# A hybrid decoder trunk on one core: all row loads ahead of the first panels, and a first pair in the order of its operands

## The chip, the cores and the metric

The kernel runs on one core of a Trainium2 chip. The metric is the device time in microseconds, as the median of several executions. The kernel before takes 1883.57 us (three runs, 1883.14 to 1888.67).

## The reference

Two layers over 256 tokens of width 1024, batch 1. Each sub-layer normalises, modulates by a condition c, mixes, gates and adds. What this case touches is the very beginning, the first sub-layer of layer 0:

```python
c_act = jax.nn.silu(c)
mod = c_act @ ada_w[0] + ada_b[0]                 # 6 * 1024 numbers
sh1, sc1, g1, sh2, sc2, g2 = jnp.split(mod, 6, axis=-1)
h = rms_norm(x, tok_norm[0]) * (1 + sc1) + sh1
b_gate, c_gate, v = jnp.split(h @ w_in, 3, axis=-1)   # w_in: 1024 x 3072
u = c_gate * v                                    # then a causal convolution of width 3
x = x + g1 * ((b_gate * conv(u)) @ w_out)
```

A channel mixer follows (product-key retrieval over 16384 experts), then the second layer with latent attention and a second channel mixer. They make up most of the time and are not changed.

## The kernel before

All is laid out with channels on the 128 partitions and 256 tokens along the free axis, so the activation is eight blocks of 128x256. A weight matrix comes as *panels* of 128x1024 f32 (512 KB): one panel holds the eight 128x128 blocks for 128 output channels. Products are made in float32r with a split: each panel is cast to a high part `w_hi` (ScalarE, `split_hi`, L1007) and the rest `w_lo` = panel minus high part (GpSimd, `split_lo`, L1353); the activation is split the same way into `act_hi` and `act_lo`. A panel is then 24 matmuls of 128x256: high by high, high weights by low activation, low weights by high activation. There are four raw slots, four slots for high and two for low panels. SyncE issues a panel's load when the low part of the panel four before it is made (`load`, L378).

The modulation is computed on VectorE as 1024-long dot products with silu(c): each *ada row* (128x1024 f32, 512 KB) gives 128 numbers (`ada_row`, L1429). Six slots hold the rows, so `load_ada(n, ...)` (L388) waits until row n - 6 has been used. Rows 0 to 7 give the scales sc1, rows 8 to 15 the shifts sh1; further rows come three by three among the panels.

The opening, engine by engine:

- SyncE (L448 to L468) issues c, row 0, x, the constants, rows 1 to 11, panels 0 and 1 of `conv_in`, rows 12 to 15, panels 2 and 3. Then a loop of three rows and three panels at a time.
- ScalarE (L1207 to L1237) makes silu(c), the squares of x and the root, copies the spread 1/rms, casts panels 0 and 1, multiplies the eight blocks by the gains (L1225), adds the shifts while it casts to `act_hi` (`normalise`, L1034), and casts panel 2. The shifts come in two halves of four blocks (semaphore `scaled`).
- VectorE (L1974 to L1993) takes the rows, makes the gains after row 7, the first four shifts after row 11, the last four after row 15, and then the low activation (`normalised_lo`, L1462). In the panel stage it consumes the products and takes further rows between.
- GpSimd (L1370 to L1381) multiplies x by 1/rms in two halves and then makes the low panels in order.
- TensorE (L989 to L996) bridges its waits by products of zeros (`busy`, L615). The first two panels are multiplied together by `first_pair` (L537): high and low weights by the first four blocks of `act_hi` for both panels, five products of zeros, the same for the other four blocks, and last the high weights by `act_lo`. Panels 2 to 23 follow by `full_panel` (L583), one after the other in two banks, then the output projection. `PAIRS_IN_ORDER` (L106) tells GpSimd in which stages the first two panels are multiplied as such a pair, whose low slots are free before the product is done (`pair_lo_used`).

The lines that set the opening's order on TensorE and in SyncE's queue are these:

```python
for j in range(KB // 2):
    load_ada(KB + j, j, (KB + j) % ADA)
for j in range(2):
    load_panel("conv_in", j)
for j in range(KB // 2, KB):
    load_ada(KB + j, j, (KB + j) % ADA)
...
busy(PAN[0], 50)
first_pair(norm_hi, norm_ready, 0, lambda p: wait_panel("conv_in", p), fill=5)
for j in range(2, 24):
    full_panel("conv_in", j)
```

Of the kernel before, what the change touches and what calls it, by code (L numbers as in the profile page):

```python
# [30 lines left out]
P = 128  # L31
D = 1024
KB = D // P
T = 256
# [10 lines left out]
RAW = 4  # L45
HI, LO = 4, 2
HI_LEAD = HI - 1
ADA = 6
# [56 lines left out]
MLA_ORDER = (3, 4, 5, 6, 0, 1, 2)  # L105
PAIRS_IN_ORDER = ("conv_in", "conv_out", "sel0", "mla_in", "mla_out", "sel1")  # L106
QB_ORDER = (4, 5, 0, 1, 2, 3)
# [8 lines left out]
def program(nc, xT_in, c_in, pos_in, vec_in, con_in, ada_in, pan_in, key_in, iota_in, u_in, v_in, out):  # L116
    ctx = ExitStack()
    grid = [nc.dram_tensor(f"gates_by_expert{l}", (KEYS * KEYS * P, 1), F32, kind="Internal").ap() for l in range(2)]
    with ctx:
# [257 lines left out]
        def _(sp):  # L377
# [7 lines left out]
            def load_panel(stage, j, unroll=0, it=0, width=D):  # L385
                load(pan_in, it * unroll + (DENSE[stage] + j), stage, j, unroll, it, width)
# [66 lines left out]
            for j in range(1, KB):  # L453
                load_ada(j, KB + j, j % ADA)
            for j in range(KB // 2):
                load_ada(KB + j, j, (KB + j) % ADA)
            for j in range(2):
                load_panel("conv_in", j)
            for j in range(KB // 2, KB):
                load_ada(KB + j, j, (KB + j) % ADA)  # L460
            for j in range(2, RAW):
                load_panel("conv_in", j)
# [33 lines left out]
        def _(pe):  # L496
# [39 lines left out]

            def first_pair(hi, lo, count, wait, acts=norm_act, fill=0):  # L537

                slots = []
                for half in range(2):  # L540
                    if half:
                        busy(STAT, fill)
                    pair_hi(hi, count, slots, acts, half * KB // 2, (half + 1) * KB // 2, wait if half == 0 else None)
                pair_lo(lo, count, slots, acts)

            def conv_pair():
# [445 lines left out]
            spread_rstd(1)  # L992
            busy(PAN[0], 50)
            first_pair(norm_hi, norm_ready, 0, lambda p: wait_panel("conv_in", p), fill=5)
            for j in range(2, 24):
# [10 lines left out]
        def _(act):  # L1006
# [26 lines left out]

            def normalise(n, l, s0):  # L1034

                for k in range(KB):
                    act.wait_ge(scaled, KB * (n - 1) + k + 1)
# [180 lines left out]
            nc.scalar.copy(rstd[:, T:2 * T], STAT[:, T:2 * T]).then_inc(rstd0_copied, 1)  # L1218
            for j in range(2):
                split_hi("conv_in", j)  # L1220
            act.wait_ge(gains0, 1)
# [4 lines left out]
            act.wait_ge(by_gain, KB)  # L1226
            normalise(1, 0, 0)
            split_hi("conv_in", 2)
            for it in range(2):
# [907 lines left out]
```

## Time and profile before

| | |
|---|---|
| median of three runs | 1883.57 us (1883.14, 1883.57, 1888.67) |
| the profiled execution | 1886.6 us, its span 1884.8 us |
| TensorE busy | 1866.2 us, 99% of the span |
| VectorE, ScalarE, GpSimd busy | 1492.7, 1001.2 and 783.3 us |
| transfers | 388.82 MB, mean 206 GB/s |
| TensorE's first panel product | at 32.42 us |
| end of the first stage's 24 panels | at 104.65 us |

The span is the time between the first and the last instruction that the profile holds; the execution's own time is a little longer. A panel of 24 matmuls takes 2.88 us at the full clock. PE, ACT, DVE, POOL and SP stand for TensorE, ScalarE, VectorE, GpSimd and SyncE.

### The profile page before, as it was taken

The page shows a single profiled execution, that of the slowest core. Times are in us where ns is not written, and L with a number is a line of the kernel's source. Part 1 is how long each engine was busy: PE and PEld are TensorE (multiplying, and loading weights), DVE is VectorE, ACT ScalarE, POOL GpSimd, SP SyncE. Part 2 cuts the span into 40 slices and gives each one's busy share as a digit, 9 for nine tenths or more (in the row PEclk, how much of TensorE's full clock was granted, in tenths as well). Part 3 has the DMA queues.
Part 4 walks back from the last instruction along what each step waited for, and adds up shares of the span by engine and source line. Part 5 has one row for each costly group of instructions (what it writes and reads, how often), then busy time and mean ns, then how long its engine had stood idle before and what let it go on. Part 6 is the DMA issues. An engine that isn't in the chain of part 4 may idle for free.

```text
span 1884.8 us, 37910 instructions
## 1 busy us (share of the span) xinstructions
PE 1866.2 (99%) x12642; PEld 1655.2 (88%) x12642; DVE 1492.7 (79%) x2893; ACT 1001.2 (53%) x1598; POOL 783.3 (42%) x378
## 2 busy tenths in 40 slices
PE   8999999999999999999999999999999999999999
PEld 7999998888888888887789999988888888888887
DVE  6758999999778977997765489988887678668866
ACT  4354555555555555554454645555555555555553
POOL 3877548788860000000062575487888820000000
PEclk8999999999999999999998999999999999999999
DMA  9986657898897777876632565577777776667664
GB/s 352 364 271 202 187 136 185 229 225 230 229 244 245 257 233 236 264 233 225 223 114 83 170 200 168 136 159 182 184 179 189 190 215 194 187 193 215 190 191 140
DMA packets 174340, 388.82 MB, mean 206 GB/s; under 512 B 48801, under 2 KB 84001, under 8 KB 173857
## 3 DMA queue, kind: packets, MB, share of 16 engines
q1 hardware_dynamic: 120960, 379.01, 64.0%
q0 software_dynamic: 36864, 0.15, 4.7%
q10 hardware_dynamic: 16416, 8.39, 1.6%
q8 instruction: 56, 0.92, 0.2%
q14 instruction: 44, 0.35, 0.1%
HBM read 377.92 MB, written 9.57 MB: 206 GB/s over the span
## 4 chain that ended last, share of the span: by engine, by line
PE 92%; DVE 4%; DMA 2%; ACT 1%; issue 1%; POOL 1%; DVEq 0%; SPq 0%; ACTq 0%; POOLq 0%
PE bank L673 36%; PE bank L658 18%; PE bank L663 9%; PE bank L637 6%; PE bank L642 6%; PE bank L638 6%; PE bank L692 2%; PE bank L704 1%; DMA raw<-in_v_panels 1%; PE bank L720 1%; PE bank L522 1%; PE bank L502 1%; PE bank L953 1%; PE bank L504 1%; PE bank L503 1%
## 5 line engine op out<-in xcount | busy, mean ns | idle before, releaser
L1012 ACT CAST w_hi<-raw 128x1024 fp32r<-128x1024 f32 (+1 forms) x603 | 630.5, 1046 | 327.9 <-PE bank L673 104.0
L1414 DVE TENSOR_TENSOR w_lo<-raw,w_hi 128x1024 fp32r<-128x1024 f32 x488 | 596.9, 1223 | 192.4 <-PE bank L673 88.5
L1389 POOL DMA_INDIRECT gates_by_expert<-g_t,place x256 | 504.9, 1972 | 190.0 <-DVE place L1713 76.4
L1361 POOL TENSOR_TENSOR w_lo<-raw,w_hi 128x1024 fp32r<-128x1024 f32 (+2 forms) x115 | 273.3, 2380 | 528.3 <-PE bank L673 381.4
L658 PE MATMUL bank<-act_two,w_hi 128*128 128x512 f32 x1536 | 379.3, 389 | 0.0
L658 PEld LDWEIGHTS bank<-act_two,w_hi 128*128 128x128 f32 x1536 | 288.3, 188 | 59.8
L673 PE MATMUL bank<-w_hi,wt_hi 128*128 128x512 f32 x1024 | 325.5, 398 | 1.9 <-DVE wt_lo L1676 1.2
L673 PE MATMUL bank<-w_lo,wt_hi 128*128 128x512 f32 x1024 | 317.9, 391 | 0.0
L673 PE MATMUL bank<-w_hi,wt_lo 128*128 128x512 f32 x1024 | 317.0, 390 | 0.0
L637 PE MATMUL bank<-act_two,w_hi 128*128 128x256 f32 x984 | 246.1, 288 | 0.0
L638 PE MATMUL bank<-act_two,w_hi 128*128 128x256 f32 x984 | 241.2, 283 | 0.0
L673 PEld LDWEIGHTS bank<-w_hi,wt_lo 128*128 128x128 f32 x1024 | 192.3, 188 | 41.9
L673 PEld LDWEIGHTS bank<-w_lo,wt_hi 128*128 128x128 f32 x1024 | 192.2, 188 | 41.8
L663 PEld LDWEIGHTS bank<-act_two,w_lo 128*128 128x128 f32 x1536 | 209.5, 190 | 15.0
L663 PE MATMUL bank<-act_two,w_lo 128*128 128x256 f32 x1536 | 213.9, 282 | 0.0
L673 PEld LDWEIGHTS bank<-w_hi,wt_hi 128*128 128x128 f32 x1024 | 178.1, 189 | 32.0 <-issue 4.2
L1065 ACT COPY ring_g<-bank 128x256 f32 (+1 forms) x192 | 71.7, 374 | 253.1 <-PE bank L663 245.1
L638 PEld LDWEIGHTS bank<-act_two,w_hi 128*128 128x128 f32 x984 | 188.5, 192 | 0.0
L637 PEld LDWEIGHTS bank<-act_two,w_hi 128*128 128x128 f32 x984 | 188.2, 191 | 0.0
L642 PE MATMUL bank<-act_two,w_lo 128*128 128x256 f32 x984 | 138.5, 283 | 0.0
L642 PEld LDWEIGHTS bank<-act_two,w_lo 128*128 128x128 f32 x984 | 127.2, 192 | 0.0
L1631 DVE TENSOR_TENSOR hot_b<-ib_t,iota 128x2048 bf16<-128x2048 bf16 x96 | 116.9, 1218 | 0.8 <-PE bank L704 0.8
(257 smaller groups left out, 1951.2 us busy)
## 6 DMA issues: line engine op xcount, KB each, us to landing
raw<-in_u_panels SPq DMA_DIRECT2D x256, 512.0 KB
raw<-in_v_panels SPq DMA_DIRECT2D x256, 512.0 KB
raw<-in_panels SPq DMA_DIRECT2D x81, 512.0 KB
ada<-in_ada_rows SPq DMA_DIRECT2D x56, 512.0 KB
arena<-in_ada_rows SPq DMA_DIRECT2D x40, 512.0 KB, 7.0
gates_by_expert<-zero ACTq DMA_DIRECT2D x2, 4096.0 KB, 22.2
arena<-gates_by_expert SPq DMA_DIRECT2D x32, 256.0 KB, 5.3
gates_by_expert<-g_t,place POOLq DMA_INDIRECT x256
```

What stands on the lines that cost most here:

```text
L637: pe.matmul(bank, w_hi[:, hi_slot, w], acts[0][k], start=(k == 0), stop=False)
L638: pe.matmul(bank, w_hi[:, hi_slot, w], acts[1][k], start=False, stop=False)
L642: mm = pe.matmul(bank, w_lo[:, lo_slot, w], acts[0][k], start=False, stop=(k == KB - 1))
L658: pe.matmul(bank[:, 0:2 * T], w_hi[:, hi_slot, w], act_two[:, :, a], start=(k == 0), stop=False, skip_group_check=True)
L663: mm = pe.matmul(bank[:, 0:T], w_lo[:, lo_slot, w], act_hi[:, a], start=False, stop=(k == KB - 1), skip_group_check=True)
L673: mm = pe.matmul(YB[2 * t + n][:], wt[:, par, a], (w_hi, w_lo)[v][:, slots[v], n * 512:(n + 1) * 512], start=False, stop=False, skip_group ...
L1012: nc.scalar.copy(w_hi[:, slot, 0:width], raw[:, slot, 0:width]).then_inc(hi_done, 1)
L1065: nc.scalar.copy(ring_g[:, bass.ds(slot * T, T)], bank[:, T:2 * T]).then_inc(lo_copied, 1)
L1361: pool.tensor_tensor(w_lo[:, lo_slot, 0:width], raw[:, slot, 0:width], w_hi[:, slot, 0:width].bitcast(F32), ALU.subtract).then_inc(lo_done, 1)
L1389: pool.indirect_dma_start(grid[l], bass.IndirectOffsetOnAxis(place[:, n:n + 1], 0), kept[:, n:n + 1], None, compute_op=ALU.add).then_inc(a ...
L1414: dve.tensor_tensor(w_lo[:, lo_slot, 0:width], raw[:, slot, 0:width], w_hi[:, slot, 0:width].bitcast(F32), ALU.subtract).then_inc(lo_done, 1)
L1631: dve.tensor_tensor(wide(hot_b[:, par, :]), each(ib_t, KEYS, token0), numbers(0, KEYS), ALU.is_equal)
```

## The change

SyncE issues all sixteen ada rows ahead of the first panel. ScalarE no longer casts panels 0 and 1 before it multiplies by the gains: it multiplies, normalises the first four blocks, casts panel 0, normalises the other four blocks and casts panels 1 and 2. TensorE multiplies the first two panels by a function of its own, `opening_pair`: panel 0's high weights by the high and then by the low activation, the same for panel 1, then the low weights of both. There are 56 products of zeros ahead of it instead of 50, and none within it. As this pair's low slots are now released by `pan_done`, `conv_in` leaves `PAIRS_IN_ORDER`; `first_pair` keeps its form for the other stages. The number of products, casts and loads is otherwise the same, and VectorE's and GpSimd's order too.

```diff
--- before.py
+++ after.py
@@ -103,7 +103,7 @@
 
 WIDTHS = {BASE["q_b"] + _j: 2 * Q_LORA for _j in range(6)} | {BASE["k_b"] + _j: 2 * KV_LORA for _j in range(4)}
 MLA_ORDER = (3, 4, 5, 6, 0, 1, 2)
-PAIRS_IN_ORDER = ("conv_in", "conv_out", "sel0", "mla_in", "mla_out", "sel1")
+PAIRS_IN_ORDER = ("conv_out", "sel0", "mla_in", "mla_out", "sel1")
 QB_ORDER = (4, 5, 0, 1, 2, 3)
 TWO_PI = 2.0 * np.pi
 sq_before = {1: 0, 3: TT}
@@ -452,13 +452,9 @@
             sp.dma_start(vec[:], vec_in).then_inc(s_const, 16)
             for j in range(1, KB):
                 load_ada(j, KB + j, j % ADA)
-            for j in range(KB // 2):
+            for j in range(KB):
                 load_ada(KB + j, j, (KB + j) % ADA)
-            for j in range(2):
-                load_panel("conv_in", j)
-            for j in range(KB // 2, KB):
-                load_ada(KB + j, j, (KB + j) % ADA)
-            for j in range(2, RAW):
+            for j in range(RAW):
                 load_panel("conv_in", j)
             with sp.Fori(0, 2) as it:
                 for b in range(4):
@@ -534,14 +530,35 @@
                         mm = pe.matmul(PAN[p][:, 0:T], w_hi[:, s[0], w], acts[1][k], start=False, stop=(k == KB - 1))
                     mm.then_inc(pan_done, 1)
 
-            def first_pair(hi, lo, count, wait, acts=norm_act, fill=0):
+            def first_pair(hi, lo, count, wait, acts=norm_act):
 
                 slots = []
                 for half in range(2):
-                    if half:
-                        busy(STAT, fill)
                     pair_hi(hi, count, slots, acts, half * KB // 2, (half + 1) * KB // 2, wait if half == 0 else None)
                 pair_lo(lo, count, slots, acts)
+
+            def opening_pair():
+
+                hi, lo, acts = norm_hi, norm_ready, norm_act
+                for p in range(2):
+                    slot, _, _, n = ring("conv_in", p)
+                    pe.wait_ge(evac["conv_in"], p + 1)
+                    pe.wait_ge(hi_done, n)
+                    for k in range(KB):
+                        if p == 0:
+                            pe.wait_ge(hi, k + 1)
+                        pe.matmul(PAN[p][:, 0:T], w_hi[:, slot, k * P:(k + 1) * P], acts[0][k], start=(k == 0), stop=False)
+                    for k in range(KB):
+                        if p == 0:
+                            pe.wait_ge(lo, k + 1)
+                        pe.matmul(PAN[p][:, 0:T], w_hi[:, slot, k * P:(k + 1) * P], acts[1][k], start=False, stop=False)
+                for p in range(2):
+                    _, lo_slot, _, n = ring("conv_in", p)
+                    pe.wait_ge(lo_done, n + RAW)
+                    for k in range(KB):
+                        mm = pe.matmul(PAN[p][:, 0:T], w_lo[:, lo_slot, k * P:(k + 1) * P], acts[0][k], start=False,
+                                       stop=(k == KB - 1))
+                    mm.then_inc(pan_done, 1)
 
             def conv_pair():
 
@@ -990,8 +1007,8 @@
             pe.wait_ge(s_const, 48)
             token_square_sums(1)
             spread_rstd(1)
-            busy(PAN[0], 50)
-            first_pair(norm_hi, norm_ready, 0, lambda p: wait_panel("conv_in", p), fill=5)
+            busy(PAN[0], 56)
+            opening_pair()
             for j in range(2, 24):
                 full_panel("conv_in", j)
             conv_pair()
@@ -1031,9 +1048,9 @@
                 nc.scalar.activation(rms[:, 0:TT], STAT[:, 0:TT], ACT.Sqrt, bias=eps[:], scale=1.0 / D
                                      ).then_inc(rms_ready, 1)
 
-            def normalise(n, l, s0):
-
-                for k in range(KB):
+            def normalise(n, l, s0, k0=0, k1=KB):
+
+                for k in range(k0, k1):
                     act.wait_ge(scaled, KB * (n - 1) + k + 1)
                     c = l * 48 + s0 * KB + k
                     nc.scalar.activation(act_hi[:, k * T:(k + 1) * T], act32[:, k * T:(k + 1) * T],
@@ -1216,16 +1233,17 @@
             rms_of(1)
             act.wait_ge(rstd_spread, 1)
             nc.scalar.copy(rstd[:, T:2 * T], STAT[:, T:2 * T]).then_inc(rstd0_copied, 1)
-            for j in range(2):
-                split_hi("conv_in", j)
             act.wait_ge(gains0, 1)
             for k in range(KB):
                 act.wait_ge(by_rstd, 1 + k * 2 // KB)
                 c = slice(k * T, (k + 1) * T)
                 nc.scalar.activation(act32[:, c], act32[:, c], ACT.Copy, scale=gain[:, k:k + 1]).then_inc(by_gain, 1)
             act.wait_ge(by_gain, KB)
-            normalise(1, 0, 0)
-            split_hi("conv_in", 2)
+            normalise(1, 0, 0, 0, KB // 2)
+            split_hi("conv_in", 0)
+            normalise(1, 0, 0, KB // 2, KB)
+            for j in range(1, HI_LEAD):
+                split_hi("conv_in", j)
             for it in range(2):
                 for b in range(4):
                     for j in range(3):
```

SyncE's queue at the opening, before (arena<-in_ada_rows is a row, raw<-in_panels a panel):

```order
L448 DMA crow<-in_c 128x1024
L391 DMA arena<-in_ada_rows 128x1024 [waits ada_rows_used]
L450 DMA xT<-in_xT 128x2048
L451 DMA con<-in_constants 128x256
L452 DMA vec<-in_vectors 128x164
L391 DMA arena<-in_ada_rows 128x1024 [waits ada_rows_used] x11
L382 DMA raw<-in_panels 128x1024 [waits panel_lo_ready] x2
L391 DMA arena<-in_ada_rows 128x1024 [waits ada_rows_used] x4
L382 DMA raw<-in_panels 128x1024 [waits panel_lo_ready] x2
```

and with the change:

```order
L448 DMA crow<-in_c 128x1024
L391 DMA arena<-in_ada_rows 128x1024 [waits ada_rows_used]
L450 DMA xT<-in_xT 128x2048
L451 DMA con<-in_constants 128x256
L452 DMA vec<-in_vectors 128x164
L391 DMA arena<-in_ada_rows 128x1024 [waits ada_rows_used] x15
L382 DMA raw<-in_panels 128x1024 [waits panel_lo_ready] x4
```

Panels 0 and 1 moved behind rows 12 to 15; nothing else in the queue moved.

ScalarE from the copy of 1/rms on, before (L1225 multiplies by the gains, L1039 adds the shifts and casts):

```order
L1218 COPY ring_g<-bank 128x256 [waits token_rstd_spread]
L1012 CAST w_hi<-raw 128x1024 [waits panel_multiplied,panel_landed0]
L1012 CAST w_hi<-raw 128x1024 [waits panel_multiplied,panel_landed1]
L1225 ACTIVATE ring_g<-ring_g,gain 128x256 [waits x_by_rstd_ready,first_gains_ready]
L1225 ACTIVATE ring_g<-ring_g,gain 128x256 [waits x_by_rstd_ready] x7
L1039 ACTIVATE act_two<-ring_g,mod 128x256 [waits x_scaled,x_by_gain_ready]
L1039 ACTIVATE act_two<-ring_g,mod 128x256 [waits x_scaled] x7
L1012 CAST w_hi<-raw 128x1024 [waits panel_multiplied,panel_landed2]
```

and with the change (the same lines are now L1235, L1029, L1240 and L1056):

```order
L1235 COPY ring_g<-bank 128x256 [waits token_rstd_spread]
L1240 ACTIVATE ring_g<-ring_g,gain 128x256 [waits x_by_rstd_ready,first_gains_ready]
L1240 ACTIVATE ring_g<-ring_g,gain 128x256 [waits x_by_rstd_ready] x7
L1056 ACTIVATE act_two<-ring_g,mod 128x256 [waits x_scaled,x_by_gain_ready]
L1056 ACTIVATE act_two<-ring_g,mod 128x256 [waits x_scaled] x3
L1029 CAST w_hi<-raw 128x1024 [waits panel_multiplied,panel_landed0]
L1056 ACTIVATE act_two<-ring_g,mod 128x256 [waits x_scaled] x4
L1029 CAST w_hi<-raw 128x1024 [waits panel_multiplied,panel_landed1]
L1029 CAST w_hi<-raw 128x1024 [waits panel_multiplied,panel_landed2]
```

Both casts moved behind the scaling, and the first of them between the two halves of the normalisation.

TensorE's first pair, before (L618 are the products of zeros, L522 and L523 high and low weights by the high activation, L534 high weights by the low activation):

```order
L618 MATMUL bank<-zero 128x512 x50
L522 MATMUL bank<-act_two,w_hi 128x256 [waits normalised_hi_ready,evacuated_conv_in,panel_lo_ready]
L523 MATMUL bank<-act_two,w_lo 128x256
...
L618 MATMUL bank<-zero 128x512 x5
...
L534 MATMUL bank<-act_two,w_hi 128x256 [waits normalised_split] x8
L534 MATMUL bank<-act_two,w_hi 128x256 x8
```

and with the change (L635 zeros, L550 high by high, L554 high weights by the low activation, L559 low weights):

```order
L635 MATMUL bank<-zero 128x512 x56
L550 MATMUL bank<-act_two,w_hi 128x256 [waits normalised_hi_ready,panel_hi_ready,evacuated_conv_in]
L550 MATMUL bank<-act_two,w_hi 128x256 [waits normalised_hi_ready] x7
L554 MATMUL bank<-act_two,w_hi 128x256 [waits normalised_split] x8
L550 MATMUL bank<-act_two,w_hi 128x256 [waits panel_hi_ready,evacuated_conv_in]
L550 MATMUL bank<-act_two,w_hi 128x256 x7
L554 MATMUL bank<-act_two,w_hi 128x256 x8
L559 MATMUL bank<-act_two,w_lo 128x256 [waits panel_lo_ready]
L559 MATMUL bank<-act_two,w_lo 128x256 x7
```

The pair's first product now waits for a high panel and no low one, and the 16 products with low weights moved from between the others to the end.

## Rows read from the trace of the kernel before

**Rows 1.** The page's part 4: the chain that ended last, by engine.

```profile
PE 92%; DVE 4%; DMA 2%; ACT 1%; issue 1%; POOL 1%; DVEq 0%; SPq 0%; ACTq 0%; POOLq 0%
```

**Rows 2.** Windows: length; PE, PEld, DVE, ACT, POOL busy; clock, DMA share, GB/s.

```profile
29.97:32.42 2.45, 0.00 (x1) 0.03 (x1) 2.45 (x5) 2.42 (x7) 2.08 (x1) 1.00 1.04 415
...
33.20:36.70 3.50, 3.50 (x16) 3.36 (x16) 3.27 (x10) 2.77 (x6) 0.00 (x0) 0.53 1.03 412
36.70:41.02 4.32, 4.32 (x36) 4.20 (x35) 1.49 (x5) 1.70 (x3) 2.46 (x2) 1.00 0.62 244
41.02:104.65 63.63, 63.63 (x533) 63.63 (x532) 49.28 (x95) 23.75 (x27) 52.96 (x22) 1.00 0.95 354
```

**Rows 3.** Timeline, SyncE's queue: start, duration, line, operation, count.

```profile
19.27 0.91 SPq L382 DMA_DIRECT2D raw<-in_panels  x2
20.22 4.55 SPq L391 DMA_DIRECT2D arena<-in_ada_rows  x4
24.82 0.91 SPq L382 DMA_DIRECT2D raw<-in_panels  x2
...
30.81 10.65 SPq L382 DMA_DIRECT2D raw<-in_panels  x3
```

**Rows 4.** Timeline, ScalarE: in brackets the idle time before, and its releaser.

```profile
26.20 1.06 ACT L1012 CAST w_hi<-raw 128x1024 fp32r<-128x1024 f32 x1 [8.01 <-DMA raw<-in_panels]
...
28.44 3.30 ACT L1225 ACTIVATE ring_g<-ring_g,gain 128x256 f32<-128x256 f32 x8
...
34.21 1.71 ACT L1039 ACTIVATE act_two<-ring_g,mod 128x256 fp32r<-128x256 f32 x4 [0.73 <-DVEq L1427]
...
60.78 1.05 ACT L1012 CAST w_hi<-raw 128x1024 fp32r<-128x1024 f32 x1 [5.55 <-DMA raw<-in_panels]
```

**Rows 5.** Timeline, VectorE, from the gains to the low activation.

```profile
21.58 0.17 DVE L1984 SCALAR_TENSOR_TENSOR gain<-bank,vec 128x8 f32<-128x8 f32 x1
...
23.09 1.26 DVE L1433 CUSTOM_DVE_ANT_0 arena<-arena,bank 128x1024 f32<-128x1024 f32 x1
...
24.27 1.26 DVE L1433 CUSTOM_DVE_ANT_0 arena<-arena,bank 128x1024 f32<-128x1024 f32 x1
...
26.87 0.16 DVE L1426 TENSOR_TENSOR mod<-bank,vec 128x4 f32<-128x4 f32 x1
28.77 1.22 DVE L1433 CUSTOM_DVE_ANT_0 arena<-arena,bank 128x1024 f32<-128x1024 f32 x1 [1.73 <-DMA arena<-in_ada_rows]
...
32.60 1.22 DVE L1433 CUSTOM_DVE_ANT_0 arena<-arena,bank 128x1024 f32<-128x1024 f32 x1
...
34.28 3.26 DVE L1468 SCALAR_TENSOR_TENSOR act_two<-ring_g,mod,act_two 128x256 fp32r<-128x256 f32 x8
```

**Rows 6.** Chain of waits, in the first pair and in panel 10: start, duration, what.

```profile
35.42 0.21 PE bank L523
...
36.06 1.40 PE bank L618 x5
...
39.38 1.92 PE bank L534 x16
...
66.25 0.96 PE bank L642 x8
```

**Rows 7.** Timeline, GpSimd: x by 1/rms, low panels 0 to 3, and 10.

```profile
18.34 4.77 POOL L1376 TENSOR_TENSOR ring_g<-xT,ring_g 128x1024 f32<-128x1024 f32 x2 [17.36 <-ACT ring_g L1218]
27.33 4.72 POOL L1361 TENSOR_TENSOR w_lo<-raw,w_hi 128x1024 fp32r<-128x1024 f32 x2 [4.22 <-ACT w_hi L1012]
38.56 4.79 POOL L1361 TENSOR_TENSOR w_lo<-raw,w_hi 128x1024 fp32r<-128x1024 f32 x2 [6.51 <-PE bank L523]
...
61.91 2.41 POOL L1361 TENSOR_TENSOR w_lo<-raw,w_hi 128x1024 fp32r<-128x1024 f32 x1 [0.77 <-ACT w_hi L1012]
```

**Rows 8.** Windows: TensorE alone in its zeros; all engines from 42 us on.

```profile
26.46:29.87 3.41, 3.41 (x16) 1.00 1.04 416
...
42.00:56.00 14.00, 14.00 (x119) 14.00 (x118) 11.83 (x24) 5.28 (x7) 11.16 (x6) 1.00 0.93 322
```

## The prediction

> **What bounds the kernel now.** I read the chain of waits first. Over the whole run it lies on TensorE for 92% of the span [rows 1], and the change touches only the first stage, so the question is when TensorE reaches the steady stream of projection panels, and whether it then stays in it. The windows show the opening: TensorE does nothing from 29.97 to 32.42 us, works at the lower clock from 33.20 to 36.70 (0.53 granted, 16 matmuls in 3.50 us) and at the full one to 41.02; from there 533 matmuls follow without a gap in 63.63 us [rows 2], which is 2.88 us a panel. So the first pair of panels is done at about 41.1 us, and every microsecond by which it ends sooner is gained, if the stream behind it still gets its panels in time.
>
> Before the pair stands the queue of transfers. SyncE issued panels 0 and 1 at 19.27, rows 12 to 15 from 20.22 to 24.77, panels 2 and 3 at 24.82 [rows 3]. Panel 0 was there when its cast began at 26.20 [rows 4]; row 12 started on VectorE at 28.77 after 1.73 us of waiting for its transfer, row 15 at 32.60 [rows 5]. Two transfers from 26.20 to 28.77 and three from there to 32.60 give 1.28 us each: landings follow the order of issue at 1.28 us, as the DMA engines are full (share 1.04, 415 GB/s [rows 2]). Row 15 then releases the second half of the normalised activation at 34.21 [rows 4]. In the pair itself TensorE spent 1.40 us on five products of zeros, waiting for that half, and its matmuls took 0.21 us at the low clock and 0.12 at the full one (1.92 us for 16) [rows 6].
>
> **The transfers.** The same eight transfers now stand as rows 12 to 15, panels 0 to 3. The landing times are 26.20, 27.48, 28.77, 30.05, 31.33, 32.6, 33.9, 35.2. So row 15 lands at 30.05 instead of 32.6, panel 0 at 31.33 instead of 26.20, panel 1 at 32.6, panels 2 and 3 where they were. The load of row n waits for row n - 6 to be used, so row 15 can't be issued before about 24.4, as now; that leaves 5.6 us to its landing where it had 8.1. Bounds: 30.05, if the place in the queue decides, and 32.6, if 8.1 us are needed whatever stands ahead. I take 30.05, because the 8.1 us held two more transfers of 1.28 us. Everything that SyncE issues after these eight keeps its order.
>
> **VectorE.** The first half of the shifts is done at 26.87 + 0.16, and the next row can start 0.2 us later, at 27.2. With data there a row takes 1.18 us (23.09 to 24.27) [rows 5]: starts at 27.2, 28.4, 29.6, 30.75, each after its landing. From the start of the fourth row to the release of ScalarE it was 34.21 - 32.60 = 1.6 us, so the second half is free at 32.35 instead of 34.21. The low halves of the activation (3.26 us for eight, 0.41 each [rows 5]) begin then and end at about 35.7, since the last one waits for ScalarE's last block (34.1).
>
> **ScalarE.** Its two casts (1.06 us each) leave the front. Scaling by the gains took 3.30 us from 28.44 [rows 4]; it can now begin when the gains are there (21.58 + 0.17 [rows 5]), its second half when GpSimd is through at 18.34 + 4.77 = 23.1 [rows 7], and ends at about 25.2. The first four blocks follow the first shifts: 27.1 to 28.8. Then the engine stands behind the cast of panel 0, whose data come at 31.33: this is the wait that takes the place of the old one. Cast to 32.4, four blocks (1.71 us [rows 4]) to 34.1, cast of panel 1 to 35.15. Its wait from 28.8 to 31.33 costs nothing by itself, as the second half isn't ready before 32.35 anyway.
>
> **GpSimd.** A low weight panel takes 2.36 us (4.72 for two [rows 7]): panel 0 from 32.4 to 34.8, panel 1 from 35.2 to 37.55.
>
> **TensorE.** Six more products of zeros at 16 in 3.41 us [rows 8] are 1.3 us and end at 31.25, before the 32.4 at which panel 0 is cast: they cost nothing. High products of panel 0 start at 32.45 (four at once, the others as ScalarE delivers, to 34.2), its products with the low activation follow VectorE to 35.8. Panel 1's 16 products: 1.92 us, to 37.7. Low weights last: panel 0's have been there since 34.8, 0.96 us, to 38.7; panel 1's since 37.55, to 39.65. By this sum panel 2 starts at 39.7 instead of 41.1: **1.4 us gained** at the full clock. If the low clock covers the same stretch as now, it meets the stream only from 35.8 to 36.7, where 0.9 us hold 4 matmuls instead of 7.5: 0.35 us. Between 1.4 and 1.05 I take 1.2, since the pause ahead of the pair falls from 2.45 us to 1.2.
>
> Here a rule speaks against the change. The record shows the clock at its low level 0.8 us after TensorE resumed, behind a pause of 2.45 us [rows 2]. The Trainium skill, page "TensorE: Matmul & The Clock Gate", section "HAM oscillation — how this bites in real kernels", says that bursts of matmuls with waits between them are throttled again and again, so that each burst runs cold; the new order, fed block by block from two engines, is such a case, and by it the pair gives back more than it gains. By that rule the sum is the second rival below.
>
> **The stream behind.** GpSimd's third low panel started at 38.56 [rows 7]; it now waits for panel 0's end, 38.7, so it stays. The raw slots of panels 0 and 1 are released at 34.8 and 37.55 instead of 29.7 and 32.05; SyncE issued panels 4 to 6 from 30.81 to 41.46 [rows 3]. Rows 16 to 18 stand ahead of panel 4 and take the landings up to 39.1, so panel 4, issued at 34.9, lands at 40.3 as before; panel 5, issued at 37.6, at 41.6 or a few tenths later; panel 6 is tied to GpSimd's third panel as before. The stream starts 1.4 us sooner on the same landings. The nearest row for the room that is left: panel 10 was cast from 60.78 to 61.83, right off its transfer [rows 4]; its low weights (from 61.91, 2.41 us [rows 7]) were ready at 64.3 and used from 66.25 [rows 6], so 1.95 us of room, of which 0.5 to 0.75 remain. Later panels are alike. So nothing is lost, and the gain moves through to the end, as the rest of the program is unchanged.
>
> Sum: -1.2 us. The profiled execution took 1886.6 us, 1.8 more than its span; with the change 1885.4. That execution is 3.0 above the median of the three runs shown, 1883.57, so I forecast 1883.57 - 1.2 = **1882.4 us**. A measurement of this kernel can tell about 0.3% (5.65 us) from no change; the gain is a fifth of that. The three runs themselves lie 5.5 us apart.
>
> **The rivals.** First, *the stream absorbs the gain*: the landings fall back by more than the room, TensorE waits once or twice in the panels, and the stage ends where it ended. For it: the DMA engines are 0.95 busy in this stage [rows 2], and two slots are freed 5 us later. Against: the room above. Time: 1883.6.
>
> Second, *the clock stays low through the pair*. From 35.8 on 32 matmuls would take 0.21 instead of 0.12 us: 2.9 us more, panel 2 at 42.6, 1.5 us later than before: 1885.1. It decides from about the fifteenth slow matmul on. For it: TensorE waits between blocks from 31.25 to 35.8. Against: the full clock lasted through the first 0.8 us after a longer pause, and the zeros now reach 1.3 us closer.
>
> Third, ending **slower**: *the transfers starve the stream*. Three panels and three rows are 3.15 MB in 8.64 us, 364 GB/s; that is the point from which it decides. The stage had 354 over all, with the first 14 us at 322 [rows 2, 8], and lived on panels fetched ahead. If the later release of two slots takes that stock away and 322 GB/s lasts, each three panels take 9.8 us, 1.1 more, seven times 7.9 us, less the gain of 1.2 and some 2 us of room: +4.7, 1888.3; with no room left, +6.7. Against: SyncE's wait for panel 6 stays, and the rate rises once the queue is full.
>
> Fourth, *row 15 comes late* (the bound of 32.6): VectorE and ScalarE stand as before, panel 1's chain moves 1.9 us back, and panel 2 starts at about 41.4: 1883.9.
>
> **How the numbers follow.** Forecast 0.58, absorbed 0.14, low clock 0.12, row 15 late 0.09, starved 0.07. All but the last lie within 0.3% of 1883.57; the last is beyond it in about half of its span. Of the forecast's 0.58, 0.03 is left for a larger gain that I don't see. So faster 0.03, same 0.93, slower 0.04. The range takes in the forecast's own bounds (-1.4 to -1.05), the first, second and fourth rival (up to 1885.1) and, because three runs of one kernel spread from 1883.14 to 1888.67, about 1.5 us beyond each end: 1880.5 to 1886.6.
>
> **What would show it.** In the new profile: rows 12 to 15 back to back on VectorE from 27.2; ScalarE's scaling done by 25.2, four blocks at 27.1, the cast of panel 0 off its transfer at 31.3, the last block at 34.1; zeros until 31.25; first product at 32.45; panel 2's first product at 39.7 to 40.1; then a stream without gaps and everything later by the same amount earlier. I am wrong if panel 2 starts after 41.1, if TensorE has gaps between 40 and 104 us, or if the later stages' length changes by more than 1 us.

## The result and the profile after

The changed kernel takes 1894.39 us (median of seven runs, 1890.43 to 1898.01), against 1885.61 us (seven runs, 1882.09 to 1889.75) for the kernel before. The ratio is 1.0049, 95% interval 1.0031 to 1.0066: slower by 6 to 12 us, where 1.2 us less was forecast. The profiled execution took 1896.7 us, its span is 1894.9 us.

The first pair of panels shows where it went. VectorE's timeline in the changed kernel, from the first half of the shifts to the low activation (L1486 is the old L1468; the two single rows are from narrower windows of the same view):

```profile
28.72 1.22 DVE L1451 CUSTOM_DVE_ANT_0 arena<-arena,bank 128x1024 f32<-128x1024 f32 x1 [0.16 <-issue]
...
33.65 0.16 DVE L1444 TENSOR_TENSOR mod<-bank,vec 128x4 f32<-128x4 f32 x1
33.95 7.65 DVE L1486 SCALAR_TENSOR_TENSOR act_two<-ring_g,mod,act_two 128x256 fp32r<-128x256 f32 x8
...
33.95 2.70 DVE L1486 SCALAR_TENSOR_TENSOR act_two<-ring_g,mod,act_two 128x256 fp32r<-128x256 f32 x1
...
39.15 2.45 DVE L1486 SCALAR_TENSOR_TENSOR act_two<-ring_g,mod,act_two 128x256 fp32r<-128x256 f32 x6
```

The eight low blocks took 7.65 us where they had taken 3.26 [rows 5]: the first 2.70, the second 2.65 (from 36.58), the last six 0.41 each. Nothing is shown as a wait; it is the instruction's own duration that grows. GpSimd's timeline beside it:

```profile
34.00 2.38 POOL L1379 TENSOR_TENSOR w_lo<-raw,w_hi 128x1024 fp32r<-128x1024 f32 x1 [9.36 <-ACT w_hi L1029]
36.59 2.35 POOL L1379 TENSOR_TENSOR w_lo<-raw,w_hi 128x1024 fp32r<-128x1024 f32 x1 [0.22 <-ACT w_hi L1029]
```

The first block ends 0.3 us after GpSimd's first low panel, the second 0.3 us after the second. Before, GpSimd's two low panels ended at 32.05 and the next began at 38.56 [rows 7], so the blocks from 34.28 to 37.54 had the engine idle beside them. ScalarE did what the forecast says (casts that waited for the transfer, blocks between):

```profile
28.69 1.71 ACT L1056 ACTIVATE act_two<-ring_g,mod 128x256 fp32r<-128x256 f32 x4 [2.06 <-DVEq L1445]
32.87 1.05 ACT L1029 CAST w_hi<-raw 128x1024 fp32r<-128x1024 f32 x1 [2.47 <-DMA raw<-in_panels]
33.88 1.71 ACT L1056 ACTIVATE act_two<-ring_g,mod 128x256 fp32r<-128x256 f32 x4
```

The chain of waits of the changed kernel runs through VectorE into TensorE (compare [rows 6]; start, duration, what):

```profile
33.95 5.28 DVE act_two L1486 x2
39.23 0.04 issue
39.28 2.96 PE bank L554 x7
42.23 1.71 PE bank L550 x8
43.94 1.71 PE bank L554 x8
45.65 2.18 PE bank L559 x16
```

And the windows, in the columns of [rows 2]:

```profile
34.00:39.30 5.30, 2.38 (x10) 1.41 (x10) 5.30 (x3) 4.41 (x7) 4.72 (x2) 1.00 1.02 413
39.30:46.50 7.20, 7.20 (x30) 6.54 (x31) 2.30 (x6) 0.00 (x0) 0.00 (x0) 0.53 0.42 155
...
47.83:111.56 63.73, 63.73 (x530) 63.44 (x530) 48.94 (x95) 22.94 (x26) 54.25 (x23) 1.00 0.94 353
```

TensorE made ten matmuls in 5.3 us while it waited, then the clock stood at its low level (0.53 granted from 39.3 to 46.5), and 16 products took 3.42 us instead of 1.92. Panel 2 starts at 47.7 instead of 41.1. From there the stream runs without a gap as before (63.73 us). So 6.6 of the 10.1 us between the two spans are lost before panel 2. Of the rest, 2.7 us lie far behind the change: the matmuls of 128x512 (L675, the old L658) run from 308.3 to 1796.0 us, before from 300.9 to 1785.9. Single executions of the kernels below differ there by more than that.

### The profile page after: what moved, and what is told of

Its sections match the earlier page's. It is cut to its first block, busy times and chain, and to the rows that moved or that the text cites. A ratio compares the mean times of both kernels' runs of the same rounds, so it can differ in the third digit from the quotient of the medians.

```text
span 1894.9 us, 37912 instructions
## 1 busy us (share of the span) xinstructions
PE 1873.0 (99%) x12643; PEld 1658.6 (88%) x12643; DVE 1497.3 (79%) x2893; ACT 1001.5 (53%) x1598; POOL 786.0 (41%) x378
## 4 chain that ended last, share of the span: by engine, by line
PE 84%; DVE 8%; DMA 2%; DVEq 2%; issue 1%; ACT 1%; POOL 1%; SPq 0%; ACTq 0%; POOLq 0%
PE bank L690 33%; PE bank L675 17%; PE bank L680 9%; PE bank L654 5%; PE bank L659 5%; PE bank L655 5%; DVE w_lo L1432 2%; PE bank L709 1%; DMA raw<-in_v_panels 1%; PE bank L721 1%; DVE arena L1451 1%; DVE hot_b L1649 1%; PE bank L737 1%; DMA raw<-in_u_panels 1%; PE bank L970 1%
## 5 line engine op out<-in xcount | busy, mean ns | idle before, releaser
L1029 ACT CAST w_hi<-raw 128x1024 fp32r<-128x1024 f32 (+1 forms) x603 | 630.3, 1046 | 337.2 <-PE bank L690 100.3
L675 PE MATMUL bank<-act_two,w_hi 128*128 128x512 f32 x1536 | 379.4, 389 | 0.0
L675 PEld LDWEIGHTS bank<-act_two,w_hi 128*128 128x128 f32 x1536 | 288.3, 188 | 59.9
```

Of the source, the lines that this page charges most:

```text
L675: pe.matmul(bank[:, 0:2 * T], w_hi[:, hi_slot, w], act_two[:, :, a], start=(k == 0), stop=False, skip_group_check=True)
L1029: nc.scalar.copy(w_hi[:, slot, 0:width], raw[:, slot, 0:width]).then_inc(hi_done, 1)
```

## The experiments

The theory A to test: *a VectorE instruction with two operands in SBUF does not run beside GpSimd's two-operand subtraction; it waits it out*. Rivals: ScalarE delivers the blocks late (B), the transfers (C), a slowing in proportion whatever the operands (D), or the order of the products itself. Panel 2's start on TensorE is read in each profile; it includes up to 3 us by which the opening varies between executions, told further down.

**Hold GpSimd back.** Ahead of GpSimd's first `split_lo`:

```diff
+            pool.wait_ge(norm_ready, KB)
             for j in range(24):
                 split_lo("conv_in", j)
```

> The changed kernel, with GpSimd's first low panel held back until VectorE has made all eight low blocks of the activation. Theory A (a VectorE instruction with two operands in SBUF waits out GpSimd's whole instruction; that made the eight blocks take 7.65 us instead of 3.26): the eight blocks take 3.3 us again, from 33.95 to about 37.3. GpSimd then makes the low panels from 37.3 to 42.1, and as the pair now ends on the second of them, panel 2 starts at about 43 instead of 47.8: some 4.5 us less, 1890 us. Theory B (the blocks are late because ScalarE delivers the high blocks late, between its casts): they still take about 7.6 us, and panel 2 starts at 51 or later.

Measured: 1886.34 us, ratio 1.0011 (0.9997 to 1.0026). VectorE's timeline of this run, then GpSimd's:

```profile
31.89 3.25 DVE L1487 SCALAR_TENSOR_TENSOR act_two<-ring_g,mod,act_two 128x256 fp32r<-128x256 f32 x8
```

```profile
35.23 14.32 POOL L1379 TENSOR_TENSOR w_lo<-raw,w_hi 128x1024 fp32r<-128x1024 f32 x6 [13.59 <-DVE act_two L1487]
```

The blocks take 3.25 us with ScalarE's order untouched, so B falls. TensorE now waits 0.27 us for the second low panel, inside the pair. Panel 2 starts at 41.1, sooner than the 43 expected, as the opening itself ran 2 us earlier in this execution. Keeping GpSimd idle through the 3.3 us of the blocks gave back 8.0 us between the medians (1894.39 and 1886.34), nearly the whole loss.

**Let VectorE make the two low panels**, behind its low blocks:

```diff
             normalised_lo(1, 0, 0)
+            for j in range(LO):
+                split_lo("conv_in", j)
...
-            for j in range(24):
+            pool.wait_ge(lo_done, RAW + LO)
+            for j in range(LO, 24):
                 split_lo("conv_in", j)
```

> The changed kernel, with the low panels 0 and 1 made by VectorE right behind the low activation (1.22 us each) instead of by GpSimd. Theory A: low blocks from 33.95 to 37.3, low panels done at 38.5 and 39.7; the pair: high and low activation of panel 0 by 37.5, panel 1 by 39.4 at the full clock, low weights by 41.3. Panel 2 starts at about 41.3 instead of 47.8, 6.5 us less, so 1886 to 1888 us; if the clock is low for the same stretch, up to 43.5. Theory B (late delivery by ScalarE): no better than 48. Theory C (the transfers behind the pair starve the stream, whatever the pair does): gaps on TensorE from panel 4 on, since panels 4 and 5 are loaded 2 us and 1 us later than in the changed kernel.

Measured: 1887.36 us, ratio 1.0015 (1.0000 to 1.0029). VectorE's timeline:

```profile
33.46 3.26 DVE L1487 SCALAR_TENSOR_TENSOR act_two<-ring_g,mod,act_two 128x256 fp32r<-128x256 f32 x8
36.63 2.35 DVE L1433 TENSOR_TENSOR w_lo<-raw,w_hi 128x1024 fp32r<-128x1024 f32 x2
```

Panel 2 starts at 40.8, as expected of A. The stream has a single gap, of 0.2 us at 57.3, where TensorE waits for a low panel of GpSimd, so C falls. The whole is still not faster than before.

**Take one operand out of SBUF.** ScalarE writes the first four scaled blocks into two PSUM banks that are free there; the later blocks stay in SBUF. Left out below: ScalarE's normalisation reads the same places, and VectorE's first block waits until the first four high blocks are made.

```diff
+        first32 = lambda k: ps[3 + k // 2][:, k % 2 * T:(k % 2 + 1) * T] if k < 4 else act32[:, k * T:(k + 1) * T]
...
-                nc.scalar.activation(act32[:, c], act32[:, c], ACT.Copy, scale=gain[:, k:k + 1]).then_inc(by_gain, 1)
+                nc.scalar.activation(first32(k), act32[:, c], ACT.Copy, scale=gain[:, k:k + 1]).then_inc(by_gain, 1)
...
-                    dve.scalar_tensor_tensor(out=act_lo[:, c], in0=act32[:, c], scalar=mod[:, sh + k:sh + k + 1],
+                    dve.scalar_tensor_tensor(out=act_lo[:, c], in0=src, scalar=mod[:, sh + k:sh + k + 1],
```

> The changed kernel, with the first four blocks of the scaled activation kept in PSUM, so that VectorE's first four low blocks have one operand in SBUF and one in PSUM; GpSimd's low panels run beside them as in the changed kernel. Theory A: the first four blocks take about 0.41 us each although GpSimd is busy, the fifth stands until GpSimd's instruction ends (36.4), the sixth possibly until the next one ends (39.0); all eight still end at 39 to 41. Theory D (VectorE is slowed by GpSimd in proportion, whatever its operands): the first four take over 1 us each.

Measured: 1889.93 us, ratio 1.0031 (1.0018 to 1.0045). VectorE's timeline, then GpSimd's:

```profile
32.09 1.66 DVE L1489 SCALAR_TENSOR_TENSOR act_two<-bank,mod,act_two 128x256 fp32r<-128x256 f32 x4
33.66 4.67 DVE L1489 SCALAR_TENSOR_TENSOR act_two<-ring_g,mod,act_two 128x256 fp32r<-128x256 f32 x4
```

```profile
32.36 2.40 POOL L1381 TENSOR_TENSOR w_lo<-raw,w_hi 128x1024 fp32r<-128x1024 f32 x1 [9.59 <-ACT w_hi L1030]
34.91 2.35 POOL L1381 TENSOR_TENSOR w_lo<-raw,w_hi 128x1024 fp32r<-128x1024 f32 x1 [0.15 <-ACT w_hi L1030]
```

This is the sharpest of the runs. Beside the same GpSimd instruction, from 32.36 on, the blocks with a PSUM operand run at 0.41 us; the first with both operands in SBUF stands until the instruction is through (1.38 us, from 33.66 to 35.04, with GpSimd's end at 34.76), and the next one behind the second (2.58 us, to 37.54, with GpSimd's end at 37.26). So it is an exclusion and depends on the operands, and D falls. The rows before say the same of another instruction: VectorE's work on a row, with one operand in SBUF and one in PSUM, took its usual 1.22 us at 28.77, in the middle of GpSimd's two low panels [rows 5, 7]. Which property of GpSimd's instruction matters (that it reads SBUF, or that it reads two operands) is not tested.

**Keep TensorE busy through the wait**, to price the clock:

```diff
+                    if p == 0:
+                        busy(PAN[1], 22)
```

> The changed kernel, with 22 products of zeros between panel 0's high products and its products with the low activation, where TensorE otherwise waits from 36 to 39.3. This measures the clock's part: the low blocks still end at 41.6. If the clock stays full, panel 1 and the low weights take 3.9 us instead of 6.1 and panel 2 starts at 45.5 to 46 instead of 47.8: 2 us less, about 1892.5. If the clock's fall is not due to that wait, panel 2 stays at 47.8 or comes later.

Measured: 1886.81 us, ratio 1.0018 (1.0005 to 1.0031). TensorE's timeline:

```profile
34.15 5.17 PE L637 MATMUL bank<-zero 128*128 128x512 f32 x22
39.16 1.12 PE L556 MATMUL bank<-act_two,w_hi 128*128 128x256 f32 x8
40.11 1.12 PE L550 MATMUL bank<-act_two,w_hi 128*128 128x256 f32 x8
```

VectorE's blocks still take 7.55 us and end at 39.3, but the clock stays full, and panel 2 follows 4.6 us after them; in the changed kernel 6.1 us lie between (41.6 to 47.7). The net gain is 1.5 us. It understates what the clock costs, because here all eight low products of panel 0 stand behind the zeros and the blocks (0.95 us), where the changed kernel makes seven of them from 39.28 to 42.23, mostly between the blocks. On the 32 products behind them the clock's part is 1.8 us: 5.60 us in the changed kernel (1.71 + 1.71 + 2.18), 3.84 here. The medians of this run and of the changed kernel differ by more (7.6 us) than the start of panel 2 (3.8 us, of which 2.3 is the earlier end of the blocks); the two intervals against before only touch, at 1.0031, so the zeros' gain in the whole time is not well measured.

**Undo the queue's order alone** (SyncE as before, casts and products as changed):

```diff
-            for j in range(KB):
+            for j in range(KB // 2):
                 load_ada(KB + j, j, (KB + j) % ADA)
-            for j in range(RAW):
+            for j in range(2):
+                load_panel("conv_in", j)
+            for j in range(KB // 2, KB):
+                load_ada(KB + j, j, (KB + j) % ADA)
+            for j in range(2, RAW):
                 load_panel("conv_in", j)
```

> The changed kernel with the order of the kernel before in SyncE's queue alone (panels 0 and 1 ahead of rows 12 to 15); casts and products stay in the new order. Theory A (collision of GpSimd's low panels with VectorE's low blocks): GpSimd's first low panel is made early (about 30 to 32.5), the second from about 37, when the low blocks (from 34.2 on, as row 15 lands later) are nearly done, so they take 3.3 to 5 us instead of 7.6, and panel 2 starts at 41.5 to 43.5, at least 4 us sooner than in the changed kernel, although the rows land later. If the time had been lost to something else in the new order of casts and products, panel 2 would stay at 47 or later.

Measured: 1890.13 us, ratio 1.0031 (1.0012 to 1.0049). The blocks took 5.35 us: GpSimd's second low panel began at 36.87 and the eighth block, at 37.00, stood behind it (2.57 us), one collision instead of two. Panel 2 started at 45.2, later than expected, because the clock was low in this pair too (16 products in 3.2 us). My expectation had GpSimd's panel from about 37, when the blocks are nearly done; it came 0.13 us ahead of the last block, and that cost 2.1 us.

**The change's order of products alone**, in the kernel before (`opening_pair` in place of `first_pair`, 50 zeros, none within):

```diff
-            first_pair(norm_hi, norm_ready, 0, lambda p: wait_panel("conv_in", p), fill=5)
+            opening_pair()
```

> The kernel before with the change's order of products in the first pair alone (no zeros within it, 50 ahead). No collision here: GpSimd's first two low panels end at 32. Theory A: low blocks 3.3 us; TensorE takes panel 0 with VectorE's blocks to 37.7, panel 1 and the low weights by 41.5 at the full clock, up to 43 at the low one: 0.4 to 2 us slower than before. If the order of the products costs by itself (each burst cold), panel 2 starts at 44 or later.

Measured: 1885.33 us, ratio 1.0012 (0.9998 to 1.0025). Low blocks 3.26 us, panel 2 at 42.6: 1.5 us later than before, with the clock low until the second half of panel 1. The order costs a little, by the clock, with no collision in it; it isn't the loss.

**The same with the collision brought about on purpose**, GpSimd's first low panel held until ScalarE's fifth high block:

```diff
+            pool.wait_ge(norm_hi, KB // 2 + 1)
             for j in range(24):
                 split_lo("conv_in", j)
```

> The run before this one (kernel before, the change's order of products), with GpSimd's first low panel held back until ScalarE has made the fifth high block, so that it starts beside VectorE's low blocks. Theory A: the eight low blocks take 7.6 us instead of 3.3 (4.3 more), and panel 2 starts 4.3 us later than in the run before this one, or more where the clock falls: 46 to 48. Theory D (no exclusion, the loss in the changed kernel came from elsewhere): low blocks 3.3 us; as the low panels are used last, panel 2 starts at most 1 us later.

Measured: 1893.36 us, ratio 1.0057 (1.0035 to 1.0079). VectorE's timeline, then GpSimd's:

```profile
34.34 7.46 DVE L1492 SCALAR_TENSOR_TENSOR act_two<-ring_g,mod,act_two 128x256 fp32r<-128x256 f32 x8
```

```profile
34.85 5.09 POOL L1384 TENSOR_TENSOR w_lo<-raw,w_hi 128x1024 fp32r<-128x1024 f32 x2 [12.50 <-ACT act_two L1062]
```

Panel 2 starts at 46.9, 4.3 us after that of the run before, which is the 4.2 by which the blocks grew. Rows, casts and queue are those of the kernel before; the collision alone makes the loss. GpSimd's two low panels are later here too, but they are ready at 39.94 and TensorE takes them from 45.18 on, so their own lateness costs nothing.

**One collision instead of two** (the changed kernel, only GpSimd's second low panel held until the blocks are made):

```diff
-            for j in range(24):
+            split_lo("conv_in", 0)
+            pool.wait_ge(norm_ready, KB)
+            for j in range(1, 24):
                 split_lo("conv_in", j)
```

> The changed kernel, with only GpSimd's second low panel held back until VectorE's eight low blocks are made. Half the dose: one of the eight blocks waits out one low panel (2.7 us), the others take 0.41 each, 5.4 to 5.6 us together (7.6 with two collisions, 3.3 with none). The second low panel is then ready 2.4 us behind the low blocks, so it hardly delays the pair; panel 2 starts about 2 to 3 us sooner than in the changed kernel.

Measured: 1889.08 us, ratio 1.0027 (1.0012 to 1.0042). The blocks took 5.38 us, between 3.26 and 7.65: each collision costs 2.1 to 2.3 us, a little less than GpSimd's 2.4. Panel 2 starts at 42.8, 4.9 us sooner than in the changed kernel, of which 1.8 is an earlier opening.

**A version meant to beat both.** Panel 0 is loaded and cast ahead of rows 12 to 15, its low part is made while VectorE works on rows, panel 1's by VectorE; TensorE takes both weights of panel 0 first, and panel 1's low weights last. Shown are SyncE, ScalarE and VectorE; GpSimd makes panel 0's low part and then waits for VectorE's, and `opening_pair` has nine products of zeros between the halves:

```diff
-            for j in range(KB):
+            for j in range(KB // 2):
+                load_ada(KB + j, j, (KB + j) % ADA)
+            load_panel("conv_in", 0)
+            for j in range(KB // 2, KB):
                 load_ada(KB + j, j, (KB + j) % ADA)
...
-            normalise(1, 0, 0, 0, KB // 2)
             split_hi("conv_in", 0)
+            normalise(1, 0, 0, 0, KB // 2)
...
             normalised_lo(1, 0, 0)
+            dve.wait_ge(lo_done, RAW + 1)
+            split_lo("conv_in", 1)
```

> A version meant to beat both. Panel 0 is loaded, cast and split ahead of rows 12 to 15, while VectorE works on rows (one operand in SBUF, one in PSUM, so no collision); panel 1's low part is made by VectorE behind its low blocks. TensorE takes panel 0's high and low weights with the high blocks as they come, with nine products of zeros between the halves, then the low blocks as they come, with panel 1's high products between, and panel 1's low weights last. Theory A: low blocks 3.3 us, from about 32.5 to 36; panel 2 starts at 38.8 to 40 instead of 41.1, so 1 to 2 us less than the kernel before, 1883 to 1884 us, at the edge of what can be measured. If anything else was at work in the changed kernel's opening, panel 2 starts after 41.

Measured: 1887.61 us against 1886.64, ratio 1.0006 (0.9994 to 1.0018): no difference. In the profile the blocks took 3.26 us and panel 2 started at 40.4, though this execution's opening ran late (1/rms was copied at 19.6, against 17.8 in the profile before). It is the earliest panel 2 of all, and not measurably faster. No version here beats the kernel before.

Side by side, by the start of panel 2 in each profile:

| kernel | low blocks, us | 1/rms copied | panel 2 | ratio |
|---|---|---|---|---|
| before | 3.26 | 17.8 | 41.1 | 1 |
| meant to beat both | 3.26 | 19.6 | 40.4 | 1.0006 |
| VectorE makes the lows | 3.26 | 18.9 | 40.8 | 1.0015 |
| GpSimd held back | 3.25 | 16.4 | 41.1 | 1.0011 |
| products only | 3.26 | 17.7 | 42.6 | 1.0012 |
| one held | 5.38 | 17.5 | 42.8 | 1.0027 |
| zeros within | 7.55 | 16.7 | 43.9 | 1.0018 |
| four blocks in PSUM | 6.24 | 17.5 | 44.8 | 1.0031 |
| queue back | 5.35 | 18.2 | 45.2 | 1.0031 |
| collision only | 7.46 | 17.1 | 46.9 | 1.0057 |
| changed | 7.65 | 19.3 | 47.7 | 1.0049 |

(6.24 is from the start at 32.09 to the end at 33.66 + 4.67.) The time follows panel 2 roughly. It stays open why all of them lie above what the shift of panel 2 gives, by 0.6 us (zeros within) to 4.9 us (collision only: 5.8 us of shift, 10.7 of time). For seven of the ten the shift lies in the run's interval; for VectorE's lows, one held and collision only it lies below, and all err to one side. One profile of each can't tell, because executions of one kernel spread by 10 us, and the part after panel 2 spreads too. Two runs whose panel 2 lies 0.3 us apart (GpSimd held back, VectorE makes the lows) had profiled spans of 1882.3 and 1890.8 us, and both began the matmuls of 128x512 at 301.2 us: the whole difference arose behind that, as they ended them at 1783.4 and 1791.9. Over the eleven profiles this stretch takes 1482.2 to 1490.7 us, in no order of panel 2.

## Why the prediction was wrong

**The queue** held. Panel 0 was late for ScalarE (2.47 us of waiting, then cast at 32.87, forecast 31.33), rows 12 to 15 were there before VectorE wanted them. In the runs with this queue whose 1/rms was copied by 17.5 (GpSimd held back, zeros within, four blocks in PSUM, one held) the cast began at 31.2 to 31.3, as forecast.

**VectorE's rows** started at 28.72 instead of 27.2. The square sums ended later in this execution: TensorE began them at 11.26 instead of 10.74, and its clock was low from 12 us on. What waits on 1/rms is held up on every engine; over the runs the copy of 1/rms lies between 16.4 and 19.6. I took one profile's phase of the clock for a fixed time. That is 1.5 us. The change doesn't make this variation, but it lays it open. In the four kernels with panels 0 and 1 ahead of the rows, row 12 started at 28.63 to 28.82 wherever 1/rms lay (17.1 to 18.2), as VectorE waited 1.3 to 2.3 us for its transfer. In the six with all rows ahead it went with 1/rms: 26.5 to 26.9 in the four with 1/rms by 17.5, then 28.23 (18.9) and 28.72 (19.3, the changed kernel). So 27.2 was within the range, and this profile is a late one.

**The low blocks** are the step that failed: "The low halves of the activation (3.26 us for eight, 0.41 each [rows 5]) begin then and end at about 35.7", beside "panel 0 from 32.4 to 34.8, panel 1 from 35.2 to 37.55" for GpSimd. I moved GpSimd's two low panels from a place where VectorE worked on rows to one where it works on low blocks, and priced both as if alone. [rows 5, 7] show the two kinds of work apart in time, so 3.26 us was a duration without a neighbour. This is 4.4 us. From the blocks' end to panel 2 it then took 6.1 us (41.6 to 47.7) where the forecast has 4.0 (35.7 to 39.7): 2.1 more, with the clock low: 32 products took 5.60 us instead of 3.84, which is 1.8 of it, and the zeros within the wait brought back 1.5 net. 1.5 + 4.4 + 2.1 make the 8.0 us between the forecast's 39.7 and 47.7.

A rule stood ready. The Trainium skill, page "GPSIMD Engine Reference", section 1, "Specifications", says that GpSimd's SBUF interfaces are shared with VectorE, with contention for VectorE instructions in a 2-port mode or with two SBUF inputs. The traces agree for two SBUF inputs (no 2-port mode is shown here), and give the size: the VectorE instruction takes 2.70 us instead of 0.41, the whole rest of GpSimd's.

**ScalarE and GpSimd** kept to the forecast, 1.5 us later by the opening: four blocks at 28.69, casts and last block as listed, low panels 2.38 and 2.35 us long.

**The clock.** The second rival (32 matmuls at 0.21, 2.9 us, chance 0.12) was right as to place: 32 of them took 5.6 us instead of 3.84. In the changed kernel it came behind the collision's wait, and with zeros in that wait the clock stayed full. It doesn't need the collision, though: in the kernel before with the new order of products alone, with low blocks of 3.26 us, the clock was low too (0.51 granted from 33.0 to 39.7). (That panel 2 started at 42.6 there, the time that this rival names, is chance: the blocks ended 1.7 us later than the forecast had them.) With VectorE's lows, panel 1's 16 products ran at the full clock (0.96 us for eight) in the same order. So the low clock hung on more than this one wait, and 0.12 was a low chance for it. The rule that the prediction takes from the Trainium skill, page "TensorE: Matmul & The Clock Gate", section "HAM oscillation — how this bites in real kernels", agrees with this trace: 0.53 was granted behind the wait with ten matmuls in 5.3 us.

**The stream behind** held entirely: no gap, so the first and third rival fell; and rows 12 to 15 were worked on back to back, at 28.72, 29.87, 31.05 and 32.23, so a late row 15 fell too. With VectorE's lows, where the stream starts at 40.8, it had one, of 0.2 us. Of the three signs of being wrong that the prediction names, the first came (panel 2 after 41.1) and so did the third: from panel 2 to the end it is 1847.2 us instead of 1843.7, mostly behind 300 us, where other runs differ as much.

**The slower rival I named** was starvation of the transfers. The one that came was on the two engines whose work I had moved side by side.

**The chances.** I gave 0.93 to no change, on the ground that a change within 10 us of opening can't move 5.65. That holds for what it can save; what it can lose has no such bound.

## What to carry to other kernels

When a step moves on GpSimd, list which VectorE instructions now run beside it, and count those with two operands in SBUF as waiting until GpSimd's current instruction is through: one collision for each GpSimd instruction, at nearly its full length. That is shown here for one pair, `scalar_tensor_tensor` on 128x256 beside a subtraction on 128x1024. A duration read from a trace is good only beside the neighbours it had. If the overlap can't be avoided, keep one operand in PSUM, or give both jobs to VectorE (1.2 us a low panel here, where GpSimd takes 2.4).

## What the runs showed that I had not expected

The exclusion leaves no wait in the profile: VectorE is shown busy for 2.70 us with a 0.41 us instruction, and the engine's total rises. A group whose longest instruction is far above its median (0.47 and 2.70 us in one group here) is the sign to look for. The recorded starts don't tell which of the two goes first: the block that stood for 2.70 us has its start at 33.95, GpSimd's instruction at 34.00. GpSimd's own instruction was longer where blocks were already running, 2.60 us in the run with the collision alone and 2.55 with zeros within, against 2.38; whether it waits for them in turn is not tested.

GpSimd kept idle through the 3.3 us of the blocks makes the whole kernel faster by some 8 us against the changed one (1886.34 against 1894.39).

TensorE's clock in the opening differs from one execution to the next, and the whole opening moved by up to 3 us between them. The window from 12 to 16 us of TensorE alone, in the kernel before (busy time, its matmuls, granted clock):

```profile
12.00:16.00 4.00, 4.00 (x22) 0.58 1.03 416
```

The same window in the changed kernel:

```profile
12.00:16.00 4.00, 4.00 (x21) 0.50 1.03 419
```

The granted clock is 0.58 and 0.50, both near the lower of the two levels (1.2 GHz). I take the difference for one between executions, not for one of the change: the run with GpSimd held back has the same opening as the changed kernel up to there, and its copy of 1/rms lies at 16.4 where the changed kernel has 19.3.
